# Picks from normalised rows, modulation behind the fourth expert, and the combine stage with both norms in one pass

## The reference, cut to what matters

```python
n2 = rms_norm(h, norm2_gain)          # h / sqrt(mean(h*h) + eps) * gain
h = h + hier_moe(n2, ...)             # 32 experts, each token goes to 2 of them
h = rms_norm(h, final_gain)

# hier_moe, per expert, on the rows that were routed to it:
hid = silu(xb @ w_gate[e]) * (xb @ w_up[e])
out = hid @ w_down[e]                 # times the token's routing weight, added to its row

# convolution layer, and the dilated layer in the same way:
mod = silu(c) @ w_mod + b_mod         # shift, scale, gate
hn = rms_norm_2(x, g) * (1 + scale) + shift
b_gate, c_gate, xin, z = split(hn @ w_in, 4)
x = x + gate * ((b_gate * conv(c_gate * xin) * silu(z)) @ w_out)
```

## Time and profile before

| | |
|---|---|
| median of three runs | 1589.2 us (1586.65 to 1589.4) |
| the profiled execution's own time | 1582.81 us |
| its span, first to last instruction | 1580.7 us |
| TensorE busy | 1430.3 us (90%) |
| VectorE busy | 705.8 us (45%) |
| ScalarE busy | 488.0 us (31%) |
| HBM read | 312.62 MB |
| mean granted TensorE clock | 0.967 of full speed |

### The profile page before, as it was taken

How to read it: one execution, slowest core, us unless ns; L and a number is a source line. 1 busy time by engine, 2 the same in 40 slices (tenths; PEclk the granted TensorE clock), 3 DMA queues, 4 the chain that set the end, 5 groups by cost and what they waited for, 6 DMA issues and landing times.

```text
span 1580.7 us, 17982 instructions
## 1 busy us (share of the span) xinstructions
PE 1430.3 (90%) x6858; PEld 994.2 (63%) x6858; DVE 705.8 (45%) x1297; ACT 488.0 (31%) x723; POOL 39.9 (3%) x73
## 2 busy tenths in 40 slices
PE   6999997999998978999639999989999999999986
PEld 5887786444443433443128888767888888888765
DVE  4468737311011021110266655545266566656545
ACT  6462523110110000111152222334354444544532
POOL 2000000000000000000111000000000000000000
PEclk9999997999999999999969999989999999999988
DMA  8837435699999994999865553201212121221101
GB/s 358 322 131 247 170 118 213 276 425 426 427 426 425 427 398 163 416 426 427 351 250 195 182 195 120 107 29 54 107 59 101 54 107 54 75 86 53 54 1 66
DMA packets 36810, 336.87 MB, mean 213 GB/s; under 512 B 4560, under 2 KB 4688, under 8 KB 18384
## 3 DMA queue, kind: packets, MB, share of 16 engines
q1 hardware_dynamic: 29632, 304.69, 47.9%
q0 software_dynamic: 6624, 29.89, 5.3%
q10 hardware_dynamic: 432, 0.60, 0.1%
HBM read 312.62 MB, written 22.54 MB: 212 GB/s over the span
## 4 chain that ended last, share of the span: by engine, by line
PE 45%; DMA 2%; DVE 2%; ACT 2%; issue 1%; POOL 0%; DVEq 0%; SPq 0%; ACTq 0%; POOLq 0%; PEld 0%; PEldq 0%
PE ps L304 43%; DMA ring<-in_wts_dram 2%; PE ps L741 1%; ACT ar L883 1%; DVE b_NL L1316 0%; PE ps L310 0%; DVE ar L1308 0%; DMA ar<-y_scratch,rt 0%; ACT b_NH L892 0%; DVE ar L1982 0%; DVE ar L1267 0%; DVE hres L1792 0%; DMA y_scratch<-gate 0%; POOL ar L2058 0%; ACT ar L1237 0%
## 5 line engine op out<-in xcount | busy, mean ns | idle before, releaser
L304 PE MATMUL ps<-ring,ar 128*64 128x512 f32 x832 | 186.0, 595 | 11.5 <-issue 5.6
L304 PE MATMUL ps<-b_NH,b_WH 128*128 128x512 f32 x704 | 186.8, 401 | 9.7 <-DVE b_NL L1316 5.0
L304 PE MATMUL ps<-b_NH,b_WL 128*128 128x512 f32 x704 | 181.3, 394 | 0.0
L1249 DVE TENSOR_TENSOR b_WL<-ring,b_WH 128x1024 fp32r<-128x1024 f32 x112 | 136.6, 1220 | 92.9 <-ACT b_WH L835 92.9
L304 PE MATMUL ps<-b_NL,b_WH 128*128 128x512 f32 x704 | 174.2, 390 | 0.0
L304 PE MATMUL ps<-ar 128*64 128x512 f32 (+5 forms) x782 | 160.9, 471 | 11.7 <-DVE ar L1612 6.8
L835 ACT ACTIVATE b_WH<-ring 128x1024 fp32r<-128x1024 f32 x112 | 118.1, 1055 | 161.6 <-PE ps L304 159.8
L1677 DVE TENSOR_TENSOR ar<-ar,ps 128x256 f32<-128x256 f32 x34 | 14.3, 422 | 328.9 <-ACT ar L1026 326.9
L304 PEld LDWEIGHTS ps<-b_NH,b_WH 128*128 128x128 f32 x704 | 130.6, 190 | 38.0 <-ACT b_NH L892 9.9
L304 PEld LDWEIGHTS ps<-b_NH,b_WL 128*128 128x128 f32 x704 | 133.8, 190 | 28.0
L304 PEld LDWEIGHTS ps<-b_NL,b_WH 128*128 128x128 f32 x704 | 132.7, 189 | 27.6
(11 more groups left out here) (269 smaller groups left out, 1876.8 us busy)
## 6 DMA issues: line engine op xcount, KB each, us to landing
ring<-in_wts_dram SPq DMA_DIRECT2D x84, 2048.0 KB, 14.0
ar<-in_wts_dram SPq DMA_DIRECT2D x24, 2048.0 KB, 20.3
spare<-in_wts_dram SPq DMA_DIRECT2D x24, 2048.0 KB, 22.9
ring<-in_wmod_dram SPq DMA_DIRECT2D x24, 512.0 KB, 4.7
ar<-in_wmod_dram POOLq DMA_DIRECT2D x24, 512.0 KB, 3.8
y_scratch<-gate POOLq DMA_DIRECT2D x11, 1024.0 KB, 21.5
y_scratch<-gate SPq DMA_DIRECT2D x44, 128.0 KB, 20.0
y_scratch<-ar SPq DMA_DIRECT2D x24, 128.0 KB, 21.2
```

Of the source, the lines that this page charges most:

```text
L304: return pe.matmul(o, l, m, start=start, stop=stop, skip_group_check=True)
L1249: dve.tensor_tensor(chunk_dst(ops[3], c, feat), chunk_src(i, n), f32(chunk_dst(ops[2], c, feat)), ALU.subtract).then_inc(S["lo"], 1)
```

## The change

1. The rounded part `xhi` and the rest `xlo` are made of rows that are already scaled by `rs`. `weigh`, `factors`, the factor copies and the second factor of `scale_x` are gone. After the experts VectorE divides by `rs` again (`root_m`).
2. The first modulation's reduction moves on TensorE from before the first pick to behind expert 3 (`N_MOD`). Ring slot 3 is free only then. Until then seven slots are used, and panel 18 is the first in slot 3.
3. The first expert starts on two of the four picks.
4. The second block picks in float32r, 64 output partitions wide, into two banks; its picks are made ahead of the expert's gated product; the picks for expert n+4 and the transposition of the hidden rows stand inside it, between its own steps.
5. The twelve branches for further blocks stand inside one `If(n_over > 0)` on all engines.
6. Combine: the second norm's factor comes from the rows before the first one. With h the summed row, VectorE sums h*h*gain*gain (`products`), and both norms together are one factor; `final_gain` goes into the modulation's scale columns (`fgc`). The residual's own norm (`normed`) is applied later, during the first panel.
7. `turned_shift` uses four buffers in both layers.

The diff, cut to its core:

```diff
-C_..., C_PW, N_COLS = ..., 113, 145
+C_..., C_PW, C_FG, N_COLS = ..., 113, 145, 153
+P_MID, N_MOD = P_MOE + 18, 3
...
-        for i in range(P_MOE + 8, P_C0):
+        for i in range(P_MOE + 7, P_MID):
+            settle(i, place[i - 7])
+        settle(P_MID, 3)
+        for i in range(P_MID + 1, P_C0):
             settle(i, place[i - 8])
...
             t.then_inc(S["rt_pe"], 1)
-            pe.wait_ge(S["md"], 24)
-            mod_columns(acc0)
-            mod_gate(acc0, (1, 6))
...
             def pick_third(b):
                 for p in range(4):
-                    for m, v in enumerate((f32(xhi[:, p, :]), f32(xlo[:, p, :]))):
-                        first, end = p + m == 0, p + m == 4
-                        mm(ps[0:64, b, :], OH3[:, p, :], v[:, 0:512], first, end)
-                        t = mm(ps[64:128, b, :], OH3[:, p, :], v[:, 512:1024], first, end)
+                    for m, v in enumerate((xhi, xlo)):
+                        for c in range(2):
+                            t = mm(ps[0:64, b + c, :], OH3[:, p, :], v[:, p, 512 * c:512 * c + 512], p + m == 0, p + m == 4)
...
+            def main_pick(n):
+                if n + 4 < NE:
+                    pe.wait_ge(S["m_oh"], n // 4 + 2)
+                    pe.wait_ge(S["m_xt"], 4 + n)
+                    pick(n % 4, 7, (xhi, xlo)).then_inc(S["m_gx"], 1)
...
-                    pick_third(3).then_inc(S["t_gx"], 1)
+                    pick_third(0).then_inc(S["t_gx"], 1)
+                    main_pick(n)
                     pe.wait_ge(S["t_xg"], n + 1)
                     turn_third(6).then_inc(S["t_tx"], 1)
+                    main_turn(n)
                     pe.wait_ge(S["t_xt"], n + 1)
...
+                if n == N_MOD:
+                    pe.wait_ge(S["t_y"], n + 1)
+                    pe.wait_ge(S["md"], 24)
+                    mod_columns(acc0)
+                    mod_gate(acc0, (1, 6))
...
-            for j in range(NOV):
-                with pe.If(n_over > j):
+            with pe.If(n_over > 0):
+                for j in range(NOV):
+                    with pe.If(n_over > j):
+                        overflow(j)
...
-                act.activation(xhi[:, p, :], hres[:, p, :], ACT.Copy).then_inc(S["xh"], 1)
+                act.wait_ge(s_un[p], U_RT + 5)
+                act.activation(xhi[:, p, :], hres[:, p, :], ACT.Copy, scale=rs[:, p:p + 1]).then_inc(S["xh"], 1)
...
-                dve.tensor_tensor(xlo[:, p, :], hres[:, p, :], f32(xhi[:, p, :]), ALU.subtract).then_inc(S["xl"], 1)
+                dve.scalar_tensor_tensor(out=xlo[:, p, :], in0=hres[:, p, :], scalar=rs[:, p:p + 1],
+                                         in1=f32(xhi[:, p, :]), op0=ALU.mult, op1=ALU.subtract).then_inc(S["xl"], 1)
...
+                dve.tensor_scalar(hres[:, p, :], hres[:, p, :], root_m[:, p:p + 1], None, ALU.mult).then_inc(S["hb"], 1)
...
+            def products(p):
+                dve.wait_ge(s_un[p], U_PK + 3)
+                dve.tensor_scalar(eps_s[:, p:p + 1], rs[:, p:p + 1], EPS / D, EPS * EPS, ALU.mult, ALU.add)...
+                dve.tensor_tensor_reduce(out=x0c[:, p, :], in0=x0c[:, p, :], in1=fgsq, scale=1.0, scalar=0.0,
+                                         op0=ALU.mult, op1=ALU.add, accum_out=rs2[:, p:p + 1])...
...
             def shifted(k):
-                    o, src = tmps[k % 2], ps[:, k, :]
+                    o, src = tmps[k % 4], ps[:, k, :]
...
-                    if k >= 2:
-                        act.wait_ge(S["nl"], nb + k - 1)
+                    if k >= 4:
+                        act.wait_ge(S["nl"], nb + k - 3)
...
                 if m == 1: ...
+                if (n, m) == (N_MOD, 1):
+                    sp.wait_ge(S["mp"], 3)
+                    load(P_MID)
```

More of the change, by code:

```diff
@@ L606, in tensor_program, with main_turn @@
             pe.wait_ge(S["xl"], 4)
-            pick(0, start_banks[0], (xlo,)).then_inc(S["m_gx"], 1)
-            pe.wait_ge(S["m_fac"], 1)
-            factors(2).then_inc(S["m_row"], 1)
-            for u in range(1, 4):
+            for u in range(2):
                 pick(u, start_banks[u], (xlo,)).then_inc(S["m_gx"], 1)
-            pe.wait_ge(S["ctl"], 1)
-            n_over, third = read_ctl(pe)
+            def main_pick(n):
[3 more added lines that the diff above has]
+                    pick(n % 4, 7, (xhi, xlo)).then_inc(S["m_gx"], 1)
+            def main_turn(n):
+                pe.wait_ge(S["m_hh"], n + 1)
+                if n:
+                    pe.wait_ge(S["m_ht"], n)
+                turn_h(hh, 4).then_inc(S["m_d1"], 1)
             for n in range(NE):
@@ L617, in tensor_program @@
                 landed(ua)
-                pe.wait_ge(S["m_xt"], 4 * g + 4)
+                pe.wait_ge(S["m_xt"], 4 * g + 4 if n else 2)
                 if n:
@@ L623, in tensor_program @@
                     down_main(n - 1)
+                else:
+                    for u in range(2, 4):
+                        pick(u, start_banks[u], (xlo,)).then_inc(S["m_gx"], 1)
+                    pe.wait_ge(S["ctl"], 1)
+                    n_over, third = read_ctl(pe)
+                    pe.wait_ge(S["m_xt"], 4)
                 landed(ub)
@@ L1080, in scalar_program @@
             result(NE - 1)
-            for j in range(NOV):
-                with act.If(n_over > j):
-                    third_block(NE + j)
+            with act.If(n_over > 0):
+                for j in range(NOV):
+                    with act.If(n_over > j):
+                        third_block(NE + j)
             hi(P_C0, 0)
@@ L1846, in vector_program @@
                         t = 4 * c + j
+                        if q == 0 and c == 0:
+                            normed(j)
+                        if q == 0 and t == 3:
+                            for p in range(4):
+                                dve.wait_ge(s_un[p], U_PK + 13)
+                            dve.memset(TT[:, :, 0:1], 0.0).then_inc(S["tt0"], 1)
+                            dve.memset(TT[:, :, 513:514], 0.0).then_inc(S["tt0"], 1)
                         if q == 1:
@@ L2045, in gpsimd_program @@
             n_over, third = read_ctl(pool)
-            for j in range(NOV):
-                with pool.If(n_over > j):
-                    pool.wait_ge(S["ty"], 32 * (NE + j + 1))
+            with pool.If(n_over > 0):
+                for j in range(NOV):
+                    with pool.If(n_over > j):
+                        pool.wait_ge(S["ty"], 32 * (NE + j + 1))
             pool.wait_ge(S["ovx"], 1)
@@ L2107, in sync_program @@
                 load(i)
-            sp.wait_ge(S["mp"], 3)
-            load(P_MOE + 7)
             sp.wait_ge(S["ctl"], 1)
@@ L2119, in sync_program @@
             for q, (n, m) in enumerate(used):
-                i = P_MOE + q + 8
-                if i < P_C0:
-                    load(i)
-                if P_MOE + q == former[P_C0]:
-                    load(P_C0)
+                for i in range(P_MOE + 7, P_C0 + 1):
+                    if former[i] == P_MOE + q:
+                        load(i)
                 if m == 1:
```

377 lines of the change are left out of this document (183 added, 194 removed).

## The result

| | before | after |
|---|---|---|
| median of the runs | 1589.0 us of 4 (1586.65 to 1589.4) | 1561.3 us of 4 (1558.93 to 1567.34) |
| the profiled execution's own time | 1582.81 us | 1559.57 us |
| its span | 1580.7 us | 1557.8 us |
| TensorE busy | 1430.3 us | 1411.8 us |

The fourth run of before, 1588.82, moves its median from 1589.2 to 1589.0. The ratio is 0.9835 (95% interval 0.9803 to 0.9866): 27.7 us less in the medians, 23.2 us less between the two profiled executions. I had said 22.2 less and 1567.0, in a range from 1555 to 1579. The four steps can be read against the new trace.

A forecast was written before the change was run, and what follows sets the result against it. Experts were taken as bound by the load stream, the stage behind by TensorE's side, dense layers by TensorE. 3.9 - 12.8 - 10.7 - 2.6 = -22.2 took the median from 1589.2 to 1567.0 us, range 1555 to 1579.

The forecast's parts named there:

- Term 1: Start of the load stream: lost slot costs 5.1 us, earlier expert 1 gives back 1.1; net +3.9, bounds -4.9 and +6.
- Panel 18: Load stream in the experts: this panel's load is issued near 336 with DMA share still 1.0, costed at nothing.
- rival (c): Experts: the moved modulation leaves TensorE at half clock, so the change turns slower, 1620 us; chance 0.03.
- Term 2: The two second blocks: each shortens from 19.7 to 14.5 us, closing the stream's gap; -12.8 us, bounds +18 and -19.
- 2 x 5.2: Second blocks: both blocks save the same 5.2 us each; with 2.4 between them, 12.8 us.
- rival (a): Second block's picks run at float32 pace, each block 10.2 us longer than forecast: 1587.4 us; chance 0.06.
- Term 3: Combine and shift: one branch instead of twelve, earlier unit rows, four shift buffers; -10.7 us, bounds -4 and -14.
- Rival (b): Combine: branches aren't what keeps TensorE; only the shift's rounds remain, about 6 of 10.7 us: 1571.7; chance 0.13.
- Term 4: Dilated layer: the same four shift buffers; -2.6 us, bounds 0 and -5.
- (d): Behind the combine: VectorE's added passes hold the first convolution panel, 1572 us; chance 0.08.
- (e): Second blocks: the stream's gap closes further, as both blocks' waits and low clock go too, 1561 us; chance 0.10.

The follow-up runs named there:

- the float32 run: The changed kernel with the sixteen picks of a second block read as float32 in the same form: 1578.4 us, ratio 0.9939.
- the flat kernel: The changed kernel with TensorE's twelve branches flat again, without the one If around them: 1563.9 us, ratio 0.9822.

## Why the prediction was right, step by step

- **Term 1** (+3.9, came as +4.7). The 5.1 us of the slot held. The 1.1 us that expert 1's half 1 was to come earlier did not: it starts 47.9 us behind the router's end, before 47.5. (The two make 5.5; the other traces with this code show 5.0 to 6.3 over before's 308.6.) I had named VectorE as what holds the first gated product, but counted only what it sheds. It shed more, in fact: the end of the modulation left this place too, 1.6 us from 280.20 in the trace before. The product still came only 0.8 us earlier behind the router's end (38.4, before 39.3). I had not counted that all the rest ahead of it on VectorE stays, so that TensorE's whole 3.5 us of lead turns into a wait with low clock behind it. The run with the weights' chain moved shows the size, 3.4 us. The upper bound of +6 doesn't follow from the two terms, which give 5.1 at most.
- **Panel 18 and rival (c).** Issued at 338.4, forecast 336; DMA share 1.0. The clock fell for one window and came back. No slow turn of the experts. (By its own rows, 26 us against 15.27, rival (c) should have read 6 x 10.7 - 25 = 39 us and 1606, not 1620.)
- **Term 2** (-12.8, came as -11.1). The block is 14.3 us, forecast 14.5; its picks take 3.77 us for sixteen, 0.236 each, forecast 0.227. The step that failed is "2 x 5.2". It took block 20 to be a copy of block 19. Block 19 is the first user of the shared place and block 20 the second, and it waits for the first one's store. It cost 3.1 us of wait above block 19's and 1.6 of low clock; with the place separate 4.6 us came back. Before, this wait couldn't be seen, since the longer block covered it (the two stores landed 12.2 and 14.9 us after their issue near 586, and the scaling came only behind 611), as the float32 run shows again. That the term is off by 1.7 us only, and not by 4.6, is luck: block 20 before was 1.7 us longer than the 19.7 I took for it, by its low clock, and the stretch between the blocks shrank by 3.4, not 2.4 (a wait of 0.80 went too). The upper bound of +18 is wrong as a sum: two blocks at the float32 pace, 20.4 by rival (a), make -12.8 + 20.4 = +7.6.
- **Term 3** (-10.7, came as -12.1). The mechanism was right and the parts add up: 6.1 us for the four buffers, 2.7 to 3.0 for the branches (the flat kernel takes 52.8 us from the last down panel to the leading panel's end, the changed one 50.1), the rest, some 3 us, for the norms in one factor, which wasn't tried by itself. The banks were full 6.8 us behind the last gathered result (798.8 to 805.57), forecast 5.9; the panel ended 21.6 behind it, forecast 22.5. What was wrong is the weight on the branches. I wrote that nothing else stands between TensorE and the turn. Removing them moved the turn from 32 to 25.6 us of waiting, and the panel's end by 3 only. The unit rows were the next to be late. Rival (b) is wrong in its cause, since flat branches bring the "issue" back. But the branches weigh less than I gave them: without their gain rival (b) left 6 of term 3's 10.7 us, and in fact 9.4 of 12.1 are left.
- **Term 4** (-2.6, came as -3.4; 3.4 also in the run with two buffers).
- **Rivals (d) and (e).** Neither came. The leading panel begins 1.4 us behind the full banks, so VectorE's added passes don't hold it. And the median lies where (e) put it, but the stream's gap was 13.2 us and not less than forecast. What (e) said of the low clock in the blocks was right (1.7 us, block 20); the store's wait took more than that back.
- **The sum.** -22.2 forecast, -22.9 in the spans. The medians differ by 27.7, with an interval from 21 to 31 us. Part of the difference is that the profiled execution of before lay 6.2 us below its median, that of after 1.8 below. I had carried the first over unchanged to the forecast. That the sum of the spans is so near is in part luck as well: terms 1 and 2 came 2.5 us short, terms 3 and 4 2.2 us over, and scatter before the router and behind the dilated panel, +1.8 and -2.8, nearly cancels.

## What to carry over

An earlier start is worth only what the next engine can take up: list what stands ahead of its first product on that engine, and move what nobody waits for behind it. Where a buffer is shared between a store and the next round's operand, cost the second round apart from the first, and count the queue that the store is in, not the store. What a branch that is not taken costs can go with the length of its body; put one branch around a row of rare cases, but read from the next engine's rows how much of the gap is really the branches'.

## What the hardware showed that I had not expected

- Twelve untaken branches over bodies of 148 and 172 instructions held TensorE for 26.4 and 32.1 us; twelve over bodies of one wait took less than the 20.8 us that it waited anyway. With the long bodies 5 to 7 more blocks of 16.4 KB of instructions were fetched.
- Two small stores issued from 586.45 on landed 16.8 and 18.5 us later, behind 2 MB loads in the same queue. Over the execution the stores of the experts' results take 25 to 27 us from issue to landing in the median.
- Waits of 2.2 and 3.5 us on TensorE were each followed by products at low clock that cost another 1.6 to 1.7 us (8.78 against 7.09, 5.27 against 3.65). Without the wait, the clock stayed at 1.00 in both places. But the length of a wait alone doesn't tell: in the kernel before, products behind a wait of 3.32 us (block 19) ran at 1.00 and behind one of 3.31 us (block 20) at 0.54.
- Rounded picks with 64 weight columns run at 0.236 us per 512 columns, the same form in float32 at 0.86, 3.7 times that.
